# First attention of block 1: each head's scores made by themselves, with the value products between the two heads

## The chip, the cores and the metric

The kernel runs on one core of one Trainium2 chip. The metric is device time in microseconds (us) of one execution, taken as the median of several runs. The core has a matmul engine (PE, with PEld for its weight loads), a vector engine (DVE), a scalar engine (ACT), GpSimd (POOL) and a queue for transfers (SP). They run their own instruction streams in order and meet at semaphores.

## The reference, cut to what matters

The program computes a first transformer block (with three mixing branches) and two further layers, in float32, for 512 tokens of width 1024. The change lies in branch "a" of the first block: attention in a window, with 8 query heads of width 64 that share 2 key heads, over blocks of 128 queries. A block of queries sees 256 context keys, and of the sequence its own block of 128 keys and its neighbours, masked to a distance of 128, and one "sink" score per head:

```python
s_loc = jnp.einsum('bnqkgd,bnjkd->bkgnqj', qb, kb).astype(jnp.float32) * scale
s_loc = jnp.where(valid, s_loc, NEG_BIG)
s_ctx = jnp.einsum('bnqkgd,bjkd->bkgnqj', qb, ck).astype(jnp.float32) * scale
p = jax.nn.softmax(jnp.concatenate([s_ctx, s_loc, s_sink], axis=-1), axis=-1).astype(v.dtype)
o = (jnp.einsum('bkgnqj,bjkd->bnqkgd', p[..., :n_ctx], cv)
     + jnp.einsum('bkgnqj,bnjkd->bnqkgd', p[..., n_ctx:n_ctx + 3 * BLOCK], vb))
```

## The kernel before, in words

The program is a row of stages. In a stage each engine has its stream, written by hand as a Python function (`tensor`, `scalar`, `vector`, `gpsimd`), and the order of the calls in it is the order on the engine. `paired_attention` makes one such stage. `attend("A", ...)` (windowed) is the stage that the change touches, `attend("B", ...)` (every query sees all 768 keys) comes straight after it with the same function, and a third use of the function, `slots=2`, is the latent attention of the later layers.

A unit `u` is a pair of heads (g = 0 and 1) and one block tb of 128 queries; there are 4 pairs and 4 blocks, so 16 units, `u = 4 * pair + tb`. The pair's two heads lie in partitions 0 to 63 and 64 to 127 of the queries `qkA` and keys `kA`. For A, units with tb = 0 or 3 have 512 keys and one masked block (narrow units here), units with tb = 1 or 2 have 640 keys and two masked blocks (wide units). Per unit:

- `scores(u)` on PE: for each range of key columns one matmul of head 0 and one of head 1, in turn, into eight banks' first half: head 0 has PSUM banks 0 and 1, head 1 has banks 2 and 3. There is room for one unit, so it waits until both heads' exponentials of the unit before are done. One semaphore step, `scored`, tells of both heads.
- `maxima(u)` on DVE: for head 0 and then head 1, add the mask (line 1163), put the sink score in (line 1165), take the row maximum (line 1167).
- `exps(u)` on ACT: exponential and row sum of head 0, then of head 1 (line 1139), out of the banks into `probsA`.
- `inverses(u)` on DVE (line 1172) waits for both exponentials; POOL then scales both heads' probabilities (line 1210).
- `transposes(u)` on PE (line 1092) turns the probabilities into banks 4, 5, 6, and `copies` brings them to `probsTA`: banks 4 and 6 by ACT (line 1144), bank 5 by DVE (line 1129).
- `values(u)` on PE (line 1105) waits for all three copies, and multiplies with the values into bank 7. After the fourth unit of a pair DVE reads bank 7 out (line 1179).

The streams are, for each u in turn: PE `scores(u+1)`, `values(u-1)`, `transposes(u)`; DVE `inverses(u)`, `maxima(u+1)`, after a pair's first unit the readout of the pair before, then its copy of unit u; ACT `exps(u+1)`, then its two copies of unit u.

Of the kernel before, what the change touches and what calls it, by code (L numbers as in the profile page):

```python
# [121 lines left out]
def build_program(nc, stream, xT_in, ctxT_in, memT_in, pos_in, const_in, axial_in, par1_in, par2_in, out):  # L122
    stack = ExitStack()
    with stack:
# [33 lines left out]
        def p1(name, n=1, at=0):  # L158
            return par1[:, PAR1[name] + at:PAR1[name] + at + n]
# [882 lines left out]

            stage(name, tensor=tensor, scalar=scalar, vector=vector, gpsimd=gpsimd)

        def paired_attention(name, pairs, unit_of, read_out, work, slots, turn_banks, out_banks, copier, sink=None):


            units = [unit_of(t, tb) for t in range(pairs) for tb in range(TB)]
            N = len(units)
            G = len(turn_banks)  # L1050
            scored = Signal("scored", N)
            max_ready = Signal("max_ready", 2 * N)
            exp_done = Signal("exp_done", 2 * N)
            inverse_ready = Signal("inverse_ready", N)
# [18 lines left out]
            def tensor(pe):  # L1073
                def scores(u):
                    if u >= slots:
                        pe.wait_ge(exp_done.sem, exp_done.at(2 * (u - slots + 1)))
                    for lo, hi, operands in units[u]["scores"]:
                        for g in range(2):
                            lhsT, rhs = operands[g]
                            last = nc.tensor.matmul(head_scores(u, g)[:, lo:hi], lhsT, rhs, start=True, stop=True)  # L1080
                    last.then_inc(scored.sem, 1)

                def transposes(u):
                    keys = units[u]["keys"]
                    for b in range(G):
                        if u > 0:
                            pe.wait_ge(probs_out[b].sem, probs_out[b].at(u))
                        for n, x in enumerate(turned_tiles(u, b)):
                            g, j = divmod(x, keys)
                            if j == 0:  # L1090
                                pe.wait_ge(probs_ready.sem, probs_ready.at(2 * u + g + 1))
                            last = nc.tensor.transpose(bank[:, turn_banks[b], n * P:(n + 1) * P],
                                                       probs[:, u % 2, g, j * P:(j + 1) * P], con("ident"))
                        last.then_inc(turned[b].sem, 1)

                def values(u):
                    t, tb = divmod(u, TB)
                    if tb == 0 and t >= len(out_banks):
                        pe.wait_ge(sum_read.sem, sum_read.at(t - len(out_banks) + 1))
                    for b in range(G):  # L1100
                        pe.wait_ge(probs_out[b].sem, probs_out[b].at(u + 1))
                    keys = units[u]["keys"]
                    for j, sides in enumerate(units[u]["values"]):
                        for g in range(2):
                            last = nc.tensor.matmul(bank[g * HD:(g + 1) * HD, out_banks[t % len(out_banks)], tb * P:(tb + 1) * P],
                                                    sides[g], probsT[:, u % 2, (g * keys + j) * P:(g * keys + j + 1) * P],
                                                    start=j == 0, stop=j == keys - 1)
                    if tb == TB - 1:
                        last.then_inc(summed.sem, 1)

                scores(0)
                if slots == 2:
                    scores(1)
                for u in range(N + 1):
                    if u + slots < N:
                        scores(u + slots)
                    if slots == 1 and u >= 1:
                        values(u - 1)
                    if u < N:
                        transposes(u)  # L1120
                    if slots == 2 and u >= 1:
                        values(u - 1)
# [32 lines left out]

            def vector(dve):
                def maxima(u):
                    dve.wait_ge(scored.sem, scored.at(u + 1))
                    unit = units[u]
                    for g in range(2):  # L1160
                        S = head_scores(u, g)
                        for lo, mask in unit["masks"]:
                            nc.vector.tensor_tensor(S[:, lo:lo + P], S[:, lo:lo + P], mask, ALU.add)
                        if sink:
                            nc.vector.tensor_copy(S[:, unit["width"] - 1:unit["width"]], sink(u // TB, g))
                            dve.drain()
                        nc.vector.tensor_reduce(stat[:, u % 2, 0, g:g + 1], S[:, 0:unit["width"]], AX.X, ALU.max, negate=True)\
                            .then_inc(max_ready.sem, 1)

                def inverses(u):  # L1170
                    dve.wait_ge(exp_done.sem, exp_done.at(2 * (u + 1)))
                    nc.vector.reciprocal(stat[:, u % 2, 2, :], stat[:, u % 2, 1, :]).then_inc(inverse_ready.sem, 1)  # L1172

                def dve_copies(u):
                    copies(dve, "dve", u, nc.vector.tensor_copy)

                def turn_out(t):
                    dve.wait_ge(summed.sem, summed.at(t + 1))
                    nc.vector.tensor_copy(read_out(t), bank[:, out_banks[t % len(out_banks)], :]).then_inc(sum_read.sem, 1)

                nc.vector.memset(stat[:, :, :, :], 0.0)
                dve.drain()
                maxima(0)
                if slots == 2:
                    inverses(0)
                    maxima(1)
                    for u in range(N):
                        if u + 1 < N:
                            inverses(u + 1)
                        if u + 2 < N:  # L1190
                            maxima(u + 2)
                        dve_copies(u)
                        if u % TB == 1 and u > TB:
                            turn_out(u // TB - 1)
                else:
                    for u in range(N):
                        inverses(u)
                        if u + 1 < N:
                            maxima(u + 1)
                        if u % TB == 0 and u:  # L1200
                            turn_out(u // TB - 1)
                        dve_copies(u)
                turn_out(pairs - 1)
# [1091 lines left out]
        def attend(which, b, windowed, qk, k, v):  # L2295

                with ExitStack() as a:
                    work = (same_place(f"probs{which}", "hcT", [P, 2, 2, ALLT], F32), tmp(f"probsT{which}", [P, 2, 2 * ALLT], a),
                            tmp(f"stat{which}", [P, 2, 3, 2], a))

                    def unit_of(n, tb):
                        lo, hi = (max(0, tb - 1), min(TB, tb + 2)) if windowed else (0, TB)
                        width = CT + (hi - lo) * P
                        key_cols = [(0, CT, 0), (CT, min(width, 512), CT + lo * P)] if lo else [(0, 512, 0)]
                        if width > 512:
                            key_cols.append((512, width, 512 + lo * P))
                        masks = []
                        if windowed and lo < tb:
                            masks.append((CT, con("mask_prev")))
                        if windowed and hi > tb + 1:  # L2310
                            masks.append((width - P, con("mask_next")))
                        blocks = list(range(CB)) + [CB + x for x in range(lo, hi)]
                        rows = [slice(g * HD, (g + 1) * HD) for g in range(2)]
                        return dict(scores=[(a0, a1, [(qk[r, n, tb * P:(tb + 1) * P], k[r, s0:s0 + a1 - a0]) for r in rows])
                                            for a0, a1, s0 in key_cols],
                                    width=width + (1 if windowed else 0), masks=masks, keys=width // P,
                                    values=[[v[:, x, r] for r in rows] for x in blocks])
                    paired_attention(f"attend{which}", 4, unit_of, lambda n: yab[:, b, n, :], work, 1, (4, 5, 6), (7,),
                                     ("act", "dve", "act"),
                                     sink=(lambda n, g: p1("sink", 1, n + 4 * g)) if windowed else None)  # L2320


        with ExitStack() as s:
# [104 lines left out]
            work = {}  # L2428
# [848 lines left out]
```

## Time and profile before

| | |
|---|---|
| median of 3 runs | 3217.31 us (3217.26 to 3220.99) |
| profiled execution, its own time | 3217.78 us |
| its span in the profile | 3216.0 us |
| PE busy | 2983.4 us, 93% of the span |
| DVE, ACT, POOL busy | 1520.6, 1281.8, 327.6 us |
| stage A | from 489.01 us (first scores) to 572.05 us (last readout ends) |
| stage B | from 572.37 us to 654.24 us |

Time in the trace is counted from the start of the span. A fp32 matmul stands in the trace as two records, and a transpose as one. Busy times of PE are modelled, so a group's duration reaches a little past the start of the next. The granted clock (PEclk) is a share of the full rate: 1.00 is 2.4 GHz, 0.50 is 1.2 GHz.

### The profile page before, as it was taken

The page shows a single profiled execution, that of the slowest core. Times are in us where ns is not written, and L with a number is a line of the kernel's source. Part 1 is how long each engine was busy: PE and PEld are TensorE (multiplying, and loading weights), DVE is VectorE, ACT ScalarE, POOL GpSimd, SP SyncE. Part 2 cuts the span into 40 slices and gives each one's busy share as a digit, 9 for nine tenths or more (in the row PEclk, how much of TensorE's full clock was granted, in tenths as well). Part 3 has the DMA queues.
Part 4 walks back from the last instruction along what each step waited for, and adds up shares of the span by engine and source line. Part 5 has one row for each costly group of instructions (what it writes and reads, how often), then busy time and mean ns, then how long its engine had stood idle before and what let it go on. Part 6 is the DMA issues. An engine that isn't in the chain of part 4 may idle for free. (4 is left out here: it accounts for less than half of the span.)

```text
span 3216.0 us, 39342 instructions
## 1 busy us (share of the span) xinstructions
PE 2983.4 (93%) x14872; PEld 2330.9 (72%) x14872; DVE 1520.6 (47%) x2141; ACT 1281.8 (40%) x1866; POOL 327.6 (10%) x285
## 2 busy tenths in 40 slices
PE   6989897899989999899899989999899899899998
PEld 2879775678768888576577768887675577678885
DVE  3346346555544442356643354442465563354432
ACT  3751334532233332434553343333434653433333
POOL 0010003500001100003000111100104001011100
PEclk8999999999999999999799999999999899999999
DMA  6100210045422222120022112222120131122222
GB/s 230 66 27 1 73 66 1 2 133 177 161 74 96 91 104 92 62 79 14 27 105 92 53 66 95 101 101 79 67 79 1 49 123 53 53 92 94 103 101 79
DMA packets 43556, 254.09 MB, mean 79 GB/s; under 512 B 4608, under 2 KB 6784, under 8 KB 15872
## 3 DMA queue, kind: packets, MB, share of 16 engines
q1 hardware_dynamic: 43392, 251.87, 21.9%
q8 instruction: 107, 1.75, 0.2%
q14 instruction: 57, 0.47, 0.0%
HBM read 249.75 MB, written 2.10 MB: 78 GB/s over the span
## 5 line engine op out<-in xcount | busy, mean ns | idle before, releaser
L238 DVE TENSOR_TENSOR ring_lo<-ring,ring_hi 128x2048 fp32r<-128x2048 f32 x201 | 460.7, 2292 | 881.5 <-ACT ring_hi L231 881.5
L289 PE MATMUL bank<-h_hi,ring_hi 128*128 128x512 f32 x1360 | 557.2, 410 | 17.2 <-DVE mix_lo L1588 6.4
L231 ACT ACTIVATE ring_hi<-ring 128x2048 fp32r<-128x2048 f32 x201 | 383.8, 1910 | 463.2 <-PE bank L289 343.3
L289 PE MATMUL bank<-h_hi,ring_lo 128*128 128x512 f32 x1360 | 534.1, 393 | 0.0
L1402 PE MATMUL bank<-h_hi,ring_hi 128*128 128x512 f32 x960 | 374.1, 390 | 5.7 <-DVE ring_lo L238 5.7
L1405 PE MATMUL bank<-h_lo,ring_hi 128*128 128x512 f32 x960 | 373.5, 389 | 0.0
L1406 PE MATMUL bank<-h_hi,ring_lo 128*128 128x512 f32 x960 | 373.5, 389 | 0.0
L289 PEld LDWEIGHTS bank<-h_hi,ring_hi 128*128 128x128 f32 x1360 | 257.2, 189 | 86.3 <-issue 22.1
L289 PEld LDWEIGHTS bank<-h_hi,ring_lo 128*128 128x128 f32 x1360 | 257.0, 189 | 60.0
L289 PE MATMUL bank<-h_lo,ring_hi 128*128 128x512 f32 x624 | 243.8, 391 | 0.0
L1402 PEld LDWEIGHTS bank<-h_hi,ring_hi 128*128 128x128 f32 x960 | 180.2, 188 | 45.3 <-issue 5.5
L289 PE MATMUL bank<-gated_lo,ring_hi 128*128 128x512 f32 x528 | 209.3, 396 | 0.0
L1406 PEld LDWEIGHTS bank<-h_hi,ring_lo 128*128 128x128 f32 x960 | 180.2, 188 | 37.5
L1405 PEld LDWEIGHTS bank<-h_lo,ring_hi 128*128 128x128 f32 x960 | 180.2, 188 | 37.4
L1510 DVE SCALAR_TENSOR_TENSOR mix<-bank,par,mix 128x511 f32<-128x511 f32 x176 | 123.8, 745 | 130.6 <-ACT mix L1466 124.3
L289 PEld LDWEIGHTS bank<-h_lo,ring_hi 128*128 128x128 f32 x624 | 117.8, 189 | 27.6 <-issue 3.9
L1466 ACT ACTIVATE mix<-bank,par 128x512 f32<-128x512 f32 x88 | 63.7, 774 | 150.2 <-PE bank L1406 150.2
L289 PE MATMUL bank<-mix_lo,ring_hi 128*128 128x512 f32 x272 | 116.5, 428 | 6.0 <-PEq L337 6.0
L289 PEld LDWEIGHTS bank<-gated_lo,ring_hi 128*128 128x128 f32 x528 | 99.2, 188 | 24.4 <-issue 2.4
L1532 POOL TENSOR_TENSOR gated<-mix 128x512 f32 (+1 forms) x44 | 57.2, 1299 | 425.9 <-ACT mix L1471 425.9
L1210 POOL TENSOR_TENSOR squares<-squares,stat 128x512 f32<-128x512 f32 x64 | 65.3, 1041 | 331.5 <-DVE stat L1172 331.5
L1510 DVE SCALAR_TENSOR_TENSOR conv<-bank,par,conv 128x511 f32<-128x511 f32 x88 | 61.9, 745 | 65.5 <-ACT conv L1466 62.4
(449 smaller groups left out, 5089.0 us busy)
## 6 DMA issues: line engine op xcount, KB each, us to landing
ring<-in_stream SPq DMA_DIRECT2D x209, 1024.0 KB, 4.8
mod_w<-in_stream SPq DMA_DIRECT2D x64, 256.0 KB, 4.8
xT<-in_xT SPq DMA_DIRECT2D x2, 2048.0 KB, 14.8
const<-in_const SPq DMA_DIRECT2D x1, 2306.5 KB, 16.0
par<-in_par SPq DMA_DIRECT2D x3, 696.0 KB, 3.9
memT<-in_memT SPq DMA_DIRECT2D x2, 1024.0 KB, 4.9
out<-xT SPq DMA_DIRECT2D x1, 2048.0 KB, 6.3
ctxT<-in_ctxT SPq DMA_DIRECT2D x1, 1024.0 KB, 4.8
```

The lines of the kernel that those rows point to most:

```text
L231: nc.scalar.activation(self.slab_hi(slab + j), self.slab(slab + j), ACT.Copy).then_inc(slab_rounded, 1)
L238: nc.vector.tensor_tensor(lower, self.slab(slab + j), self.slab_hi(slab + j).bitcast(F32), ALU.subtract)\
L289: ins = nc.tensor.matmul(out, lhsT, rhs, start=start and w is w_hi and x is x_hi, stop=stop and w is w_lo)
L1210: nc.gpsimd.tensor_tensor(p, p, stat[:, u % 2, 2, g:g + 1].to_broadcast([P, p.shape[1]]), ALU.mult)\
L1402: first = nc.tensor.matmul(out_ap[s], w_hi, x_hi, start=k == 0, stop=False)
L1405: nc.tensor.matmul(out_ap[s], w_hi, x_lo, start=False, stop=False)
L1406: last = nc.tensor.matmul(out_ap[s], w_lo, x_hi, start=False, stop=k == KT - 1)
L1466: last = nc.scalar.activation(work[:, j % 2, s, :], out_ap[s], ACT.Identity, bias=conv_b(col), scale=conv_w(2 * FT + col))
L1510: last = nc.vector.scalar_tensor_tensor(w, out_ap[s][:, 1 - lo:T - lo], conv_w(col), w, ALU.mult, ALU.add)
L1532: nc.gpsimd.tensor_tensor(gated(n), work[:, j % 2, 0, :], work[:, j % 2, 1, :], ALU.mult)\
```

## The change

With `apart` set (stage A alone), each head's scores are a step of their own, `head_alone(u, g)`. It waits only for that head's exponential of the unit before, and signals that head alone; DVE waits per head. PE's order for each u becomes: head 0 of unit u+1, values of u-1, head 1 of unit u+1, transposes of u.

```diff
-            scored = Signal("scored", N)
+            scored = Signal("scored", 2 * N if apart else N)
...
+                def head_alone(u, g):
+                    if u >= 1:
+                        pe.wait_ge(exp_done.sem, exp_done.at(2 * (u - 1) + g + 1))
+                    for lo, hi, operands in units[u]["scores"]:
+                        lhsT, rhs = operands[g]
+                        last = nc.tensor.matmul(head_scores(u, g)[:, lo:hi], lhsT, rhs, start=True, stop=True)
+                    last.then_inc(scored.sem, 1)
+
+                if apart:
+                    head_alone(0, 0)
+                    head_alone(0, 1)
+                else:
+                    scores(0)
                 if slots == 2:
                     scores(1)
                 for u in range(N + 1):
-                    if u + slots < N:
+                    if apart and u + 1 < N:
+                        head_alone(u + 1, 0)
+                    if u + slots < N and not apart:
                         scores(u + slots)
                     if slots == 1 and u >= 1:
                         values(u - 1)
+                    if apart and u + 1 < N:
+                        head_alone(u + 1, 1)
                     if u < N:
                         transposes(u)
...
-                    dve.wait_ge(scored.sem, scored.at(u + 1))
+                    if not apart:
+                        dve.wait_ge(scored.sem, scored.at(u + 1))
                     unit = units[u]
                     for g in range(2):
+                        if apart:
+                            dve.wait_ge(scored.sem, scored.at(2 * u + g + 1))
                         S = head_scores(u, g)
...
-                                     sink=(lambda n, g: p1("sink", 1, n + 4 * g)) if windowed else None)
+                                     sink=(lambda n, g: p1("sink", 1, n + 4 * g)) if windowed else None, apart=windowed)
```

On PE at the third and fourth unit of a pair, before (kA and qkA are the scores, probsTA the values, probsA the transposes):

```order
L1080 MATMUL bank<-kA,qkA 128x256 x4
L1080 MATMUL bank<-kA,qkA 128x128 x2
L1105 MATMUL bank<-probsTA,vab 64x128 x8
L1092 MATMUL bank<-const,probsA 128x128 x10
L1080 MATMUL bank<-kA,qkA 128x256 x4
L1105 MATMUL bank<-probsTA,vab 64x128 x10
L1092 MATMUL bank<-const,probsA 128x128 x10
```

and the same units with the change:

```order
L1117 MATMUL bank<-kA,qkA 128x256 x2
L1117 MATMUL bank<-kA,qkA 128x128
L1106 MATMUL bank<-probsTA,vab 64x128 x8
L1117 MATMUL bank<-kA,qkA 128x256 x2
L1117 MATMUL bank<-kA,qkA 128x128
L1093 MATMUL bank<-const,probsA 128x128 x10
L1117 MATMUL bank<-kA,qkA 128x256 x2
L1106 MATMUL bank<-probsTA,vab 64x128 x10
L1117 MATMUL bank<-kA,qkA 128x256 x2
L1093 MATMUL bank<-const,probsA 128x128 x10
```

The same matmuls are issued, but head 1's moved behind the values of the unit before. At the start of the stage PE had

```order
L1080 MATMUL bank<-kA,qkA 128x512 x4
L1080 MATMUL bank<-kA,qkA 128x128 x2
L1092 MATMUL bank<-const,probsA 128x128 x8
L1080 MATMUL bank<-kA,qkA 128x256 x4
L1080 MATMUL bank<-kA,qkA 128x128 x2
```

and has with the change

```order
L1117 MATMUL bank<-kA,qkA 128x512 x3
L1117 MATMUL bank<-kA,qkA 128x128
L1117 MATMUL bank<-kA,qkA 128x512
L1117 MATMUL bank<-kA,qkA 128x128
L1093 MATMUL bank<-const,probsA 128x128 x8
```

The first three are both heads of unit 0 and head 0 of unit 1; no values stand between the heads yet, since there is no unit before. DVE, ACT and POOL issue the same instructions in the same order as before; DVE only has one more wait in each unit.

## Rows read from the trace of the kernel before

**Rows 1.** The page: busy time, share and instructions of each engine.

```profile
PE 2983.4 (93%) x14872; PEld 2330.9 (72%) x14872; DVE 1520.6 (47%) x2141; ACT 1281.8 (40%) x1866; POOL 327.6 (10%) x285
```

**Rows 2.** Stretches of stage A: length, busy us (instructions), clock, DMA share, GB/s.

```profile
489.00:494.00 5.00, 1.93 (x6) 0.81 (x8) 2.25 (x8) 2.81 (x5) 0.57 (x1) 0.74 0.00 0
...
494.00:572.00 78.00, 59.12 (x556) 44.35 (x552) 48.97 (x141) 36.65 (x92) 35.47 (x32) 0.93 0.00 1
...
499.00:504.00 5.00, 4.46 (x29) 3.56 (x30) 2.03 (x9) 1.50 (x5) 2.47 (x2) 0.50 0.00 0
```

**Rows 3.** Who waited for whom in stage A: us, times, longest.

```profile
PE bank L1080 <- ACT probsA L1139: 19.3, 15, 3.1
DVE bank L1163 <- PE bank L1080: 20.3, 16, 2.4
```

**Rows 4.** Timeline, 520 to 536 us: start, us, engine, line, what [idle before].

```profile
520.89 0.50 DVE L1163 TENSOR_TENSOR bank<-bank,const 128x128 f32<-128x128 f32 x2 [1.24 <-PE bank L1080]
...
522.26 0.49 DVE L1163 TENSOR_TENSOR bank<-bank,const 128x128 f32<-128x128 f32 x2
...
523.74 0.80 ACT L1139 ACTIVATE probsA<-bank,statA 128x641 f32<-128x641 f32 x1 [0.42 <-DVE statA L1167]
...
524.53 0.86 ACT L1144 ACTIVATE probsTA<-bank 128x512 f32<-128x512 f32 x2
...
524.68 1.14 PE L1080 MATMUL bank<-kA,qkA 64*128 64x256 f32 x8 [1.57 <-ACT probsA L1139]
...
525.75 1.31 PE L1105 MATMUL bank<-probsTA,vab 128*64 128x128 f32 x20
525.86 0.30 DVE L1163 TENSOR_TENSOR bank<-bank,const 128x128 f32<-128x128 f32 x1 [1.03 <-PE bank L1080]
...
526.90 0.29 DVE L1163 TENSOR_TENSOR bank<-bank,const 128x128 f32<-128x128 f32 x1
...
526.99 1.31 PE L1092 MATMUL bank<-const,probsA 128*128 128x128 f32 x10
...
528.05 0.69 ACT L1139 ACTIVATE probsA<-bank,statA 128x513 f32<-128x513 f32 x1 [0.19 <-DVE statA L1167]
...
528.73 0.86 ACT L1144 ACTIVATE probsTA<-bank 128x512 f32<-128x512 f32 x2
...
532.93 0.76 ACT L1144 ACTIVATE probsTA<-bank 128x384 f32<-128x384 f32 x2
...
533.09 1.35 PE L1080 MATMUL bank<-kA,qkA 64*128 64x512 f32 x8 [0.80 <-ACT probsA L1139]
...
534.37 1.09 PE L1105 MATMUL bank<-probsTA,vab 128*64 128x128 f32 x16
534.48 0.50 DVE L1163 TENSOR_TENSOR bank<-bank,const 128x128 f32<-128x128 f32 x2 [1.25 <-PE bank L1080]
...
535.39 1.09 PE L1092 MATMUL bank<-const,probsA 128*128 128x128 f32 x8
```

**Rows 5.** Timeline, the last units of the stage.

```profile
565.64 0.69 ACT L1139 ACTIVATE probsA<-bank,statA 128x513 f32<-128x513 f32 x1 [0.19 <-DVE statA L1167]
...
566.32 0.86 ACT L1144 ACTIVATE probsTA<-bank 128x512 f32<-128x512 f32 x2
...
567.33 1.31 PE L1105 MATMUL bank<-probsTA,vab 128*64 128x128 f32 x20 [1.44 <-ACT probsTA L1144]
```

**Rows 6.** Timeline, the first units of the stage.

```profile
489.01 1.13 PE L1080 MATMUL bank<-kA,qkA 64*128 64x512 f32 x4 [1.66 <-PEq L337]
...
491.33 0.69 ACT L1139 ACTIVATE probsA<-bank,statA 128x513 f32<-128x513 f32 x1 [1.09 <-DVE statA L1167]
...
492.37 0.69 ACT L1139 ACTIVATE probsA<-bank,statA 128x513 f32<-128x513 f32 x1 [0.25 <-DVE statA L1167]
...
493.20 2.50 PE L1080 MATMUL bank<-kA,qkA 64*128 64x512 f32 x8 [3.06 <-ACT probsA L1139]
```

**Rows 7.** Timeline, latent attention: one head's scores, keys in all 128 partitions.

```profile
1502.43 1.98 PE L1080 MATMUL bank<-hT,q 128*128 128x512 f32 x4
```

More of the change, by code:

```diff
@@ L1043, in attention, with paired_attention @@
             stage(name, tensor=tensor, scalar=scalar, vector=vector, gpsimd=gpsimd)
-        def paired_attention(name, pairs, unit_of, read_out, work, slots, turn_banks, out_banks, copier, sink=None):
+        def paired_attention(name, pairs, unit_of, read_out, work, slots, turn_banks, out_banks, copier, sink=None, apart=False):
             units = [unit_of(t, tb) for t in range(pairs) for tb in range(TB)]
@@ L1109, in values @@
                         last.then_inc(summed.sem, 1)
-                scores(0)
+                def head_alone(u, g):
[10 more added lines that the diff above has]
+                    scores(0)
                 if slots == 2:
```

## The prediction

> **What bounds the kernel now.** I read the page first: PE is busy for 93% of the span and no other engine for half of it [rows 1]. The change touches stage A alone, so the second view is the busy time of that stage. There PE is busy for 59.12 of 78 us [rows 2]: it is not at its limit, and the stage is set by a chain of waits through three engines. The waits name it: PE's scores wait for ACT's exponential 15 times, 19.3 us in all, and DVE's first mask waits for PE's scores 16 times, 20.3 us [rows 3]. The timeline shows the chain [rows 4]. From a wide unit's exponential of head 1 (523.74) it goes to the next scores (524.68), from these to the first mask (525.86), through both heads on DVE (the masks start at 525.86 and 526.90) and to the next exponential of head 1 (528.05). The values (525.75) and transposes (526.99) run on PE while DVE works, and cost nothing. What follows stage A waits for its end, so what the stage loses or gains goes to the total in full.
>
> The chain in pieces, N for a narrow unit and W for a wide one. Exponential of head 1 to the next scores: 0.94 W (523.74 to 524.68), 0.83 N (492.37 to 493.20) [rows 4, 6]. Scores to mask: 1.18 N (524.68 to 525.86), 1.39 W (533.09 to 534.48). DVE's head 0: 1.04 N (525.86 to 526.90), 1.37 W (520.89 to 522.26). DVE's head 1 until ACT starts: 1.15 N (526.90 to 528.05), 1.48 W (522.26 to 523.74) [rows 4]. From one wide unit to the next this gives 0.94 + 1.39 + 1.37 + 1.48 = 5.18 us, and four units of a pair give 18.7.
>
> **What the change does, part by part.**
>
> *The two heads are no longer side by side.* A head takes 64 of the array's 128 rows. Two matmuls of 512 columns (four records), one in each half, take 1.13 us in stage A [rows 6]; the same four records with keys in all 128 rows take 1.98 us in the latent attention [rows 7]. So in stage A the halves work at once, and the difference, 0.85 us, is one whole matmul. I take it that a head by itself costs the 0.85 us (640 columns: 1.07) that both cost now, so that PE's work on scores doubles; half of that is the lower bound, and a rival below. "Scores to mask" then stays at 1.18 and 1.39 for one head.
>
> *Head 0 goes ahead.* Its scores for unit u+1 need only the exponential of head 0 of unit u, and PE has nothing else then (it waits there now). DVE can start its head 0 right behind `inverses(u)`. So DVE's head 0 (1.04 or 1.37) leaves the chain. That is the gain.
>
> *Head 1 goes behind the values of u-1.* On PE `values(u-1)` stands ahead of head 1, and it waits for the copies of u-1. ACT issues those behind both exponentials of unit u. Queued behind this wait on PE are head 1 and the transposes of u; DVE's head 1, ACT's exponential of head 1 and all that follows wait for head 1. The new chain, from exponential of head 1 to exponential of head 1, is:
> - exponential to ACT's copies: 0.68 N (528.05 to 528.73), 0.79 W (523.74 to 524.53); the two copies of the unit before take 0.76 N or 0.86 W [rows 4];
> - last copy to values: the end of the stage has this already, since no scores are left there. The copies start at 566.32 and take 0.86, the values start at 567.33, so 0.15 [rows 5];
> - values to the next group on PE: 1.02 N (534.37 to 535.39), 1.24 W (525.75 to 526.99) [rows 4];
> - scores to mask of the next unit, 1.18 or 1.39, and DVE's head 1, 1.15 or 1.48.
>
> By position in the pair (the copies and values are those of the unit before):
> - unit 0 to 1: 0.68 + 0.76 + 0.15 + 1.02 + 1.39 + 1.48 = 5.48
> - 1 to 2: 0.79 + 0.76 + 0.15 + 1.02 + 1.39 + 1.48 = 5.59
> - 2 to 3: 0.79 + 0.86 + 0.15 + 1.24 + 1.18 + 1.15 = 5.37
> - 3 to 0: 0.68 + 0.86 + 0.15 + 1.24 + 1.18 + 1.15 = 5.26
>
> Four units: 21.7 against 18.7 now. 14 of the 15 steps are of this kind: 4 x 5.59 + 4 x 5.37 + 3 x 5.26 + 3 x 5.48 = 76.1 us. The first step has no values in it. Head 0's exponential starts at 491.33 [rows 6], head 0 of unit 1 goes at 491.33 + 0.83 = 492.16, DVE has it at 493.55, head 1 at 494.92, and the exponential comes at 496.40: 4.0 us from 492.37. Together 80.1 us. Now it is 492.37 [rows 6] to 565.64 [rows 5], 73.3 us. Behind the last exponential nothing changes. The stage is **6.8 us longer**.
>
> *An array that changes its tiling once more per unit.* Values and the following group are 1.24 us apart where the values' modelled time is 1.31 [rows 4], so 0.07 overlaps; that 1.24 is in the sum. The Trainium skill ("TensorEngine Tiling (Array Packing)", Key Properties) says that changing the tiling mode drains the engine. With a full drain the step would be 1.31, and the sum 14 x 0.07 = 1.0 us more; the trace has it at 1.24, and I keep that.
>
> *The clock at the start.* PE waits 3.06 us after the first scores, and the second ones take 2.50 us [rows 6] against 1.35 later for the same shapes [rows 4]: the clock has fallen to its lower level, 1.2 GHz (0.74 on average from 489 to 494, 0.50 from 499 to 504) [rows 2]. With the change PE works for 1.7 us first, then waits some 1.3 us instead of 3.06. The sum above has the full clock throughout. So it already has in it that the half clock, which now costs two steps 1.15 us each, goes away. If the clock falls all the same, both heads of unit 1 lie one behind the other on the chain, and each takes 1.15 more: about 2.2 us on top. If it stays low for another unit, its values (1.0) and head 1 (1.15) add the next 2.1.
>
> *The rest.* DVE's added waits cost nothing: each is over when DVE comes to it, or it is head 1's, counted above. POOL's scaling starts where it did, with `inverses(u)`, and the transposes now come later than it. Transfers are idle in the stage (1 GB/s) [rows 2].
>
> **The sum.** The profiled execution took 3217.78 us and would take 3224.6. It lies 0.47 over the median of 3217.31; from that: 3217.3 + 6.8 = **3224.1 us**.
>
> **The rivals.**
> - *The clock falls anyway* (0.34). For: a wait of over 1 us is still there and PE idles before the stage. Against: it is less than half as long as the one now. 3224.1 + 2.2 = 3226.3, up to 3228.4.
> - *A head alone takes half as long as two* (0.10), if it isn't the halves working at once that the 1.13 against 1.98 shows but matmuls of 64 rows being quicker. Then "scores to mask" falls by 0.43 N and 0.53 W, over 14 steps 6.7 us, and 0.5 in the first: 6.8 - 7.2 = -0.4, 3216.9 us. Against: the Trainium skill ("TensorE: Matmul & The Clock Gate", table "Why this matters for your kernels") says that a single matmul of 32 rows takes the time of one of 128, and that the gain is the tiles' concurrency.
> - *Not slower, since the values don't stand in the way* (0.05). If the values of u-1 had run before the exponential of head 1 of unit u ended, head 1 would start at once, and PE's own row would be the limit: per narrow unit two heads of 1.07 (524.68 to 525.75) and twice 1.02, per wide unit two of 1.28 (533.09 to 534.37) and twice 1.24, or 18.4 for four against 18.8 measured. That gives some 1.3 us, with the 2.3 of the clock 3.6: 3213.7. It decides where the copies and values take 6.8 / 14 = 0.5 us less of each step. Against: ACT's copies are in its stream behind both exponentials.
> - *More is late than I count* (0.05): a transpose or readout that now holds up head 0, 0.5 us per unit: 3232.
>
> **How the numbers follow.** My forecast holds 0.46. It is a sum of 14 equal steps, so 0.1 us in a step is 1.4 in the total; its own range is 3222 to 3226.5. A measurement of this kernel tells about 0.2% from no change, 6.4 us, so the line is at 3223.7. The forecast lies close to it: 0.6 of its share is slower; of the clock rival 0.9; of the last all. 0.46 x 0.6 + 0.34 x 0.9 + 0.05 = 0.63 slower. Faster by over 6.4 us has no mechanism above, only errors of several together: 0.04. The rest, 0.33, is within. For the range I leave out the half-time rival's lower part and the last: 3217 to 3229.
>
> **What would show it.** In the changed profile: a head's scores of 512 columns in about 1.1 us and 640 in 1.3; values that start 0.15 us behind ACT's copies, with the idle time put down to them; head 1's first mask waiting for PE, head 0's not; 21.7 us per pair; PE's busy time in the stage up by about 15 us; the clock at 1.00 from 492 to 500. I am wrong if head 1's scores start right at the exponential's end, if a head's scores take half, or if DVE's head 0 still waits.

## The result, and the profile after

The changed kernel takes 3227.6 us in the median of its first eight runs, against 3217.3 (3215.3 to 3221.0) for the kernel before: 0.33% slower, with a 95% interval of 0.24 to 0.43%. Seven of the eight lie between 3225.2 and 3232.3 us (median 3227.3); the eighth, a slow one at a granted clock of 0.525, took 7940 us and is left out of the comparison. Run again beside the experiments it took 3226.0 (3225.4 to 3227.9), 0.30% slower (0.19 to 0.42).

The page of the changed kernel, its span and the busy time of the engines:

```profile
span 3226.2 us, 39342 instructions
...
PE 3002.6 (93%) x14872; PEld 2343.1 (73%) x14872; DVE 1521.2 (47%) x2141; ACT 1281.4 (40%) x1866; POOL 327.6 (10%) x285
```

Beside [rows 1]: the same instructions, and PE busy for 19.2 us more (its weight loads, PEld, for 12.2 us more). The busy times of DVE, ACT and POOL have not moved by a microsecond.

The timeline of the changed kernel, at the end of a pair and the start of the next. Line 1117 is one head's scores, 1106 the values, 1093 the transposes; on ACT line 1156 is the exponential and 1161 the copies; on DVE line 1183 is the mask.

```profile
531.70 1.31 PE L1106 MATMUL bank<-probsTA,vab 128*64 128x128 f32 x20 [1.02 <-ACT probsTA L1161]
532.11 0.69 ACT L1156 ACTIVATE probsA<-bank,statA 128x513 f32<-128x513 f32 x1 [0.55 <-DVE statA L1187]
...
532.94 1.13 PE L1117 MATMUL bank<-kA,qkA 64*128 64x256 f32 x4
...
534.00 1.31 PE L1093 MATMUL bank<-const,probsA 128*128 128x128 f32 x10
...
534.11 0.30 DVE L1183 TENSOR_TENSOR bank<-bank,const 128x128 f32<-128x128 f32 x1 [2.09 <-PE bank L1117]
...
535.24 1.12 PE L1117 MATMUL bank<-kA,qkA 64*128 64x512 f32 x2
535.26 0.69 ACT L1156 ACTIVATE probsA<-bank,statA 128x513 f32<-128x513 f32 x1 [2.38 <-DVE statA L1187]
535.94 0.86 ACT L1161 ACTIVATE probsTA<-bank 128x512 f32<-128x512 f32 x2
...
536.40 0.30 DVE L1183 TENSOR_TENSOR bank<-bank,const 128x128 f32<-128x128 f32 x1 [0.16 <-PE bank L1117]
...
536.95 1.31 PE L1106 MATMUL bank<-probsTA,vab 128*64 128x128 f32 x20 [0.59 <-ACT probsTA L1161]
...
538.19 1.12 PE L1117 MATMUL bank<-kA,qkA 64*128 64x512 f32 x2
```

Read it as a chain from 535.26. ACT's exponential of head 1 starts. Its copies start at 535.94 and end at 536.80. The values start at 536.95, 0.15 behind, and PE's idle time is put down to those copies. Head 1's scores start at 538.19, 1.24 behind the values. One head's 512 columns, two records, take 1.12 us, where both heads' four records took 1.13 in [rows 6]. DVE's mask of head 0 waits for 0.16 us (536.40), that of head 1 for 2.09 (534.11). The exponentials of head 1 come at steps of 5.48, 5.59, 5.35 and 5.25 us through a pair, 21.7 us, against 18.8 before.

Who waited for whom in stage A of the changed kernel, from 489 to 582 us (us in all, times, longest):

```profile
DVE bank L1183 <- PE bank L1117: 32.9, 24, 2.9
PEld bank L1106 <- ACT probsTA L1161: 12.1, 10, 1.8
...
PE bank L1106 <- ACT probsTA L1161: 10.7, 13, 1.6
...
PE bank L1117 <- ACT probsA L1156: 2.0, 1, 2.0
```

Beside [rows 3], PE's scores no longer wait for the exponential (19.3 us then, 2.0 now), but PE's values wait for ACT's copies (10.7 us), and DVE waits longer than before for scores (32.9 against 20.3).

The first units, and two stretches of the stage with the granted clock (the third figure from the end):

```profile
488.87 1.13 PE L1117 MATMUL bank<-kA,qkA 64*128 64x512 f32 x4 [1.66 <-PEq L337]
...
491.99 3.53 PE L1117 MATMUL bank<-kA,qkA 64*128 64x512 f32 x8 [1.99 <-ACT probsA L1156]
```

```profile
492.00:511.00 19.00, 19.00 (x79) 14.04 (x80) 8.21 (x25) 6.52 (x16) 6.97 (x6) 0.50 0.00 0
516.00:582.00 66.00, 55.94 (x434) 40.04 (x430) 37.43 (x108) 28.44 (x72) 27.73 (x25) 1.00 0.01 1
```

The first scores take 1.13 us, as before: unit 0 has one range per head, so its two matmuls stand in the same order as they did. PE still idles 1.99 us ahead of unit 1, the clock falls to 1.2 GHz near 491.3, and it stays there until about 511.6 although PE is busy in all of those 19 us. In the kernel before it was back near 505. The steps there are 5.2, 8.3 and 7.9 us, where the chain at the full clock has 4.0, 5.6 and 5.4.

From stage A's first scores to stage B's first scores it is 83.4 us before (489.01 to 572.37) and 96.5 after (488.87 to 585.33): 13.1 us longer. I call this "stage A" below. The span grew by 10.2 only. Of the difference 1.7 us comes back in a later stage whose code is the same (its place is 12.5 us late before it and 10.8 after it). The windows of that place, 13 us apart, the kernel before first:

```profile
847.00:867.00 20.00, 17.75 (x75) 14.17 (x74) 12.89 (x17) 8.67 (x12) 0.00 (x0) 0.91 0.50 189
```

```profile
860.00:880.00 20.00, 17.75 (x80) 14.24 (x80) 12.91 (x18) 9.08 (x12) 0.00 (x0) 1.00 0.49 188
```

The clock fell there for a moment before the change, and doesn't now. The rest of the program wanders by more than this: outside stage A the profiled execution has 3132.6 us before, 3129.7 in the changed kernel and 3127.2 in its second profile, and over all kernels below 3123.0 to 3134.9. So stage A itself is the better measure of each experiment.

### The profile page after: what moved, and what is told of

Read it like the earlier page. It is cut to its first block and busy times, and to the rows that moved or that the text cites. A ratio compares the mean times of both kernels' runs of the same rounds, so it can differ in the third digit from the quotient of the medians.

```text
span 3226.2 us, 39342 instructions
## 1 busy us (share of the span) xinstructions
PE 3002.6 (93%) x14872; PEld 2343.1 (73%) x14872; DVE 1521.2 (47%) x2141; ACT 1281.4 (40%) x1866; POOL 327.6 (10%) x285
```

## The experiments

Theory A, of the prediction: the values between the heads, with their wait for ACT's copies, make the chain longer than DVE's head 0 shortens it, and the low clock at the start adds to it. Theory B: the scores' doubled work on PE is the cause, wherever the values stand.

Stage A is read from the one profiled execution of each kernel, the median from all its runs; the interval compares them with runs of the kernel before made beside them.

| kernel | stage A | median, us | against before, 95% interval |
|---|---|---|---|
| before | 83.4 | 3217.3 | |
| changed | 96.5 | 3227.6 | +0.24 to +0.43% |
| changed, again | 96.5 | 3226.0 | +0.19 to +0.42% |
| both heads ahead of the values | 74.9 | 3208.1 | -0.50 to -0.23% |
| the same with a filler | 70.7 | 3205.3 | -0.52 to -0.25% |
| the same, heads staggered by one range | 72.6 | 3202.1 | -0.57 to -0.30% |
| changed with a filler | 90.0 | 3227.4 | +0.17 to +0.41% |
| before with fillers | 82.9 | 3214.9 | -0.14 to +0.04% |
| before, head after head | 87.8 | 3221.6 | +0.06 to +0.26% |
| both ahead, head 0 waits for both exponentials | 86.1 | 3216.4 | -0.12 to +0.07% |
| before, values first | 131.6 | 3263.6 (one run) | |
| changed with filler, copies between | 80.9 | 3220.2 | -0.02 to +0.20% |

### Both heads ahead of the values

```diff
                     if apart and u + 1 < N:
                         head_alone(u + 1, 0)
+                        head_alone(u + 1, 1)
...
                     if slots == 1 and u >= 1:
                         values(u - 1)
-                    if apart and u + 1 < N:
-                        head_alone(u + 1, 1)
```

> The changed kernel, but both heads' scores of unit u+1 stand ahead of the values of u-1 (head 0, head 1, values, transposes). Theory A (the values between the heads, with their wait for ACT's copies, make the chain long): the chain shrinks to 13.9 us per four units and PE's own row of 18.4 sets the pace, so stage A takes 78 us at the full clock (before 83.0, changed 96.1); if the clock stays low as long as in the changed kernel, 85 to 88. In total 3213 to 3222. Theory B (the doubled scores on PE cost the time, wherever the values stand): stage A stays at 90 or more at the full clock, 3224 or more in total.

It took 3208.1 us (3200.7 to 3208.7), 0.36% under the kernel before, and stage A 74.9 us. In the full-clock part the steps are 3.9 to 4.6 us, 16.2 for four units. Theory B's 90 us for the stage is out, since only the values have moved. But 16.2 is also under the 18.4 that I had as PE's own limit, and stage A was below the 78 expected. The timeline of this kernel shows why:

```profile
524.94 1.37 PE L1117 MATMUL bank<-kA,qkA 64*128 64x512 f32 x4
...
526.24 1.31 PE L1106 MATMUL bank<-probsTA,vab 128*64 128x128 f32 x20
...
527.48 1.09 PE L1093 MATMUL bank<-const,probsA 128*128 128x128 f32 x8
...
528.29 0.69 ACT L1155 ACTIVATE probsA<-bank,statA 128x513 f32<-128x513 f32 x1 [0.20 <-DVE statA L1186]
...
528.50 1.97 PE L1117 MATMUL bank<-kA,qkA 64*128 64x512 f32 x8
...
530.40 1.09 PE L1106 MATMUL bank<-probsTA,vab 128*64 128x128 f32 x16
```

Both heads of a narrow unit take 1.30 us from start to the values (524.94 to 526.24), not twice 1.07. When nothing stands between the heads, head 1's matmul, which uses the array's other half, runs beside the rest of head 0's. A wide unit takes 1.90 us (528.50 to 530.40), not twice 1.28; its head 1 cannot start with head 0, since it waits for ACT's exponential, which starts at 528.29 and takes 0.69. The values in between take that away as well, so this run alone does not part the values' wait from the longer scores; the run with the copies moved, below, does. From 516 to 553 PE is busy for 36.98 of 37 us. It has no idle time left, but head 1's wait still lies inside its order.

```profile
516.00:553.00 37.00, 36.98 (x317) 28.91 (x316) 29.69 (x86) 21.57 (x57) 20.47 (x18) 1.00 0.00 1
```

### The clock at the start: a filler

```diff
                 if apart:
                     head_alone(0, 0)
                     head_alone(0, 1)
+                    for _ in range(1):
+                        nc.tensor.matmul(bank[:, 7, :], con("ident"), yc[:, 0, :], start=True, stop=True)
```

The filler writes into a bank that the stage overwrites before it is read. In the changed kernel:

> The changed kernel with one matmul of 128 rows and 512 columns more, whose result nobody uses, behind the first two heads' scores, where PE idles. Theory A: of the 13.1 us that stage A is longer, 6.8 are the chain and 6.3 the clock at 1.2 GHz from 491.4 to 511.6; if the filler keeps the clock up, stage A takes 89.9 us, with a step of 5.6 from unit 1 to unit 2 instead of 8.3, and the total is 3221 to 3225. If the first steps are long for another reason than the clock, the steps stay at 5.2 and 8.3 and stage A at 96 even with the clock at 1.00. If the clock falls in spite of the filler, the run tells nothing.

The first rows of stage A in that kernel, and the clock over its whole length:

```profile
490.25 1.12 PE L1124 MATMUL bank<-yc,const 128*128 128x512 f32 x2
...
492.31 2.38 PE L1117 MATMUL bank<-kA,qkA 64*128 64x512 f32 x8 [0.94 <-ACT probsA L1158]
```

```profile
489.20:503.20 14.00, 11.80 (x64) 7.36 (x64) 9.06 (x29) 7.17 (x16) 4.51 (x4) 1.00 0.00 0
503.20:579.20 76.00, 63.04 (x498) 45.20 (x499) 42.50 (x122) 32.27 (x82) 31.54 (x28) 1.00 0.00 1
```

The clock stays up (1.00), and the first scores of unit 1 take 2.38 us where they took 3.53. The steps are 4.04, 5.58, 5.36, 5.25, 5.47 and so on, each within 0.02 us of the prediction's, and stage A takes 90.0 us, 6.7 more than before. So of the 13.1 us, 6.7 are the chain and 6.4 the low clock. The median, 3227.4 us (3222.8 to 3230.1), lies above the 3221 to 3225 expected: what stage A gave back (6.4 us) does not show in the total. In the profiled execution the rest of the program took 4.3 us more than in the changed kernel's (3134.0 against 3129.7). The stage with the clock's dip alone took 4.5 us more: its place 855 to 955 us of the kernel before lasts 102.7 us here and 98.2 in the changed kernel. Two later places, 4.9 us shorter and 5.1 us longer, nearly cancel.

In the kernel with both heads ahead of the values:

> The first kernel of this set with one filler. Theory A: with the full clock PE's row of 18.4 us per four units sets the pace: stage A 78.3 us, total 3211 to 3214, so 0.1 to 0.2% under the kernel before. Theory B: stage A 90.

Stage A 70.7 us, 3205.3 us (3204.2 to 3207.4). All steps are 3.9 to 4.5. Of the 4.3 us less in the stage, 4.1 are in the first four steps, where the low clock had been. It is 12 us, 0.38%, under the kernel before, and better than expected for the reason above.

In the kernel before, three of them behind the first `scores`:

> The kernel before with three such fillers behind the first scores of stage A (the gap there is 3.1 us). Theory A: the half clock costs the kernel before 2.3 us in its first steps, so stage A takes 80.7 us instead of 83.0 and the total is 3214 to 3216. If the clock's cost is hidden: 83.0 and no change.

Stage A took 82.9 us and 3214.9 in total (3214.6 to 3217.8), no measurable change. The first step got shorter (6.23 to 5.08 us) but the second stayed at 6.34, and one later went from 5.19 to 5.92: the clock fell later instead (1.00 from 490 to 495, but 0.86 from 495 to 500, 0.75 from 520 to 525 and 0.70 from 540 to 545). The fillers only moved it, so this run doesn't tell the price that I had named (2.3 us).

### The heads' places alone

```diff
-                    for lo, hi, operands in units[u]["scores"]:
-                        for g in range(2):
-                            lhsT, rhs = operands[g]
+                    spans = units[u]["scores"]
+                    for i, g in [(i, g) for g in range(2) for i in range(len(spans))] if sink else \
+                            [(i, g) for i in range(len(spans)) for g in range(2)]:
+                        lo, hi, operands = spans[i]
+                        lhsT, rhs = operands[g]
```

> The kernel before, but scores() of stage A issues all ranges of head 0 and then all of head 1, instead of one of each in turn; waits, the one signal and the place ahead of the values stay. It measures what is lost when the heads don't stand side by side. If matmuls of the two halves overlap only where they are next to each other in PE's order, then head 0's last range and head 1's first still overlap: units with one range per head lose nothing, units with two or three lose 0.4 to 0.9 us each, 2.1 per four units, 8 in all: stage A 91, total 3223 to 3227. If two heads in turn don't run at once at all (half-time rival): no change, 3217. If a head alone takes the full time with no overlap: 15 us more, 3232.

3221.6 us (3218.4 to 3225.7), stage A 87.8. The total is just under the range, but the mechanism that I had given, a loss in every unit with two or three ranges, is wrong in its detail. The scores of this kernel, all at the full clock, for units with two ranges (twice), and with three:

```profile
525.28 1.14 PE L1082 MATMUL bank<-kA,qkA 64*128 64x256 f32 x8 [0.17 <-ACT probsA L1141]
...
533.70 1.36 PE L1082 MATMUL bank<-kA,qkA 64*128 64x512 f32 x8 [0.80 <-ACT probsA L1141]
...
538.90 1.89 PE L1082 MATMUL bank<-kA,qkA 64*128 64x256 f32 x12 [1.80 <-ACT probsA L1141]
```

With two ranges per head the time is what it was with the heads in turn (1.14 and 1.35 in [rows 4]), although two matmuls of head 0 stand ahead of head 1's first. The trace's single records show how: two records of 512 columns start together (533.70 and 533.71), and all four come before the first of 128 columns (534.66). So head 1's first matmul ran ahead of head 0's second, which stands before it in PE's order. With three it is 1.89 against the 1.36 that the same 12 records took before: 0.5 us lost, once in four units. That is 2 us in the stage; I put the other 2.4 down to dips of the clock (0.83 from 520 to 530, 0.73 from 560 to 570, where it was 1.00 before).

### Head 0's early start alone

```diff
                 def head_alone(u, g):
                     if u >= 1:
-                        pe.wait_ge(exp_done.sem, exp_done.at(2 * (u - 1) + g + 1))
+                        pe.wait_ge(exp_done.sem, exp_done.at(2 * u))
```

on top of the kernel with both heads ahead of the values.

> The kernel with both heads ahead of the values, but head 0 too waits for both exponentials of the unit before; DVE still gets a signal per head. The doubled work on PE is there, the early start of head 0 is not. If the early start is what gave the 9.6 us of the kernel with no values between: steps as in the kernel before (5.2, 4.3, 4.2, 5.1), stage A 83, total 3216 to 3219. If it were the signal per head or the changed order: near 3208.

3216.4 us (3210.9 to 3218.9), no difference from the kernel before, and steps of 5.17, 4.30, 4.19, 5.06 where the clock is up. So neither the signal per head nor the new order gives anything; the early start of head 0 gives all of what the kernel with both heads ahead gained. Its stage A of 86.1 is 2.7 us longer than before, which I put down to lower clocks (0.63 from 500 to 510 against 0.75, and 0.66 from 540 to 545 against 1.00). The profiled execution is the fastest of its ten, 3210.9 us, by a rest of the program of 3123.0 us.

### The values' place alone

```diff
                 for u in range(N + 1):
+                    if sink and u >= 1:
+                        values(u - 1)
                     if u + slots < N:
                         scores(u + slots)
-                    if slots == 1 and u >= 1:
+                    if slots == 1 and u >= 1 and not sink:
                         values(u - 1)
```

> The kernel before with heads side by side, but with the values of u-1 ahead of the scores of u+1 in stage A (values, scores, transposes). It measures the place of the values alone. Theory A: the wait for ACT's copies and the values stand in the chain, with DVE's head 0 still in it: steps of 7.0, 6.4, 6.3, 6.9 instead of 5.2, 4.3, 4.2, 5.1, stage A 110, total 3244. If the values' place cost little and the doubled scores were the cause: below 3222.

3263.6 us in its one run, stage A 131.6. It is in the direction of Theory A and far beyond its number: the steps are 6.2 to 9.0. The chain (7.0, 6.4, 6.3, 6.9) was worked out at the full clock. Here the clock comes and goes, 0.73 on average in the stage against 0.92 before, and PE waits for ACT's copies 16 times, 41.9 us in all. How much of the miss is the clock was not measured.

```profile
548.81 1.31 PE L1105 MATMUL bank<-probsTA,vab 128*64 128x128 f32 x20 [2.68 <-ACT probsTA L1146]
550.05 1.13 PE L1080 MATMUL bank<-kA,qkA 64*128 64x512 f32 x4
...
554.99 1.98 PE L1105 MATMUL bank<-probsTA,vab 128*64 128x128 f32 x16 [2.79 <-ACT probsTA L1146]
```

The second values take 1.98 us for 16 records, 1.09 in [rows 4]: the half clock. The wait on ACT's copies is in both rows.

### The copies' place

In the changed kernel with a filler, ACT's two copies of unit u-1 go between its exponentials of unit u.

```diff
                     for g in range(2):
+                        if apart and g == 1 and u >= 1:
+                            act_copies(u - 1)
...
-                    if slots == 1:
+                    if slots == 1 and not (apart and u + 1 < N):
                         act_copies(u)
```

> The changed kernel with one filler, and with ACT's copies of unit u-1 moved between its two exponentials of unit u, so that the values don't wait for copies behind head 1's exponential. Theory A: the values start earlier, but ACT then waits for the transposes; four units take 20.3 us instead of 21.7, stage A 85, total 3220 to 3223. If the wait for the copies is not what holds the values: steps unchanged at 5.6, 5.4, 5.3, 5.5 and 3225 to 3228.

Stage A took 80.9 us, 9.1 less than the same kernel without this (90.0), with steps of 4.4 to 5.2 and 19.1 for four units, better than the 20.3 expected. The median is 3220.2, but the runs spread from 3212.9 to 3227.3, and the profiled one took 3217.7; the total can't be told from the kernel before. What holds the changed kernel is shown all the same. The order on PE is that of the changed kernel, head, values, head, with each head by itself, so its work is as large. PE is busy for 75.0 us of the stage, against 74.9 without the moved copies. Only the copies come earlier, the values hardly wait for ACT any more, and the chain is 2.5 us shorter in four units:

```profile
PE bank L1106 <- ACT probsTA L1165: 0.6, 1, 0.6
```

```profile
520.00:530.00 10.00, 10.00 (x73) 6.37 (x74) 6.28 (x18) 5.73 (x15) 4.50 (x4) 1.00 0.01 2
530.00:540.00 10.00, 9.49 (x73) 7.25 (x71) 7.32 (x21) 5.19 (x13) 4.50 (x4) 1.00 0.00 1
```

So it is the wait, and not PE's work, that sets the changed kernel's pace. But the work is close behind. Without the wait PE is busy for 19.49 of 20 us (520 to 540), and four units take 19.1 us, still not under the 18.8 of the kernel before. The kernel with both heads ahead takes 16.2, and with a filler its PE is busy for 66.7 us of the stage, since the heads overlap there. Of the 5.5 us per four units between the changed kernel and that one, 2.5 are the wait, and the other 2.9 come when the heads are neighbours.

### Staggered heads

On top of the kernel with both heads ahead and a filler: head 0's first range, then one range of each head in turn (still behind the two waits), then head 1's last. For a unit with one or two ranges per head this list is the same as without, so only the units with three ranges, one in four, change their order.

> The kernel with both heads ahead of the values and one filler (3205.3 us, four units in 16.2 us, PE never idle), but head 1 now stands one range behind head 0 in PE's order instead of a whole head: first range of head 0, then in turn a range of each, then the last of head 1. Theory A (PE sets the pace and matmuls of the two halves overlap when they are next to each other): units with two or three ranges per head take 0.4 us less on PE, so four units take 15.2 to 15.8 us, 2 to 4 us in all: 3201 to 3204. If head 1's wait for its exponential holds up head 0's second range, or the chain of 13.9 us with DVE is already the limit: no change or 1 us slower.

3202.1 us (3201.4 to 3205.7), but stage A is 72.6 us, 1.9 longer than without (70.7), with steps of 4.54, 3.30, 4.54, 4.29, 16.7 for four units. In the stage the expectation failed, and its own second case came out: head 1's wait for its exponential holds up what stands behind it. The unit with three ranges gets shorter, from its scores to its values, only from 2.51 to 2.35 us. The next unit, whose order on PE is the same, gets longer, from 1.46 (534.28 to 535.74) to 2.05 us (533.84 to 535.89). Without and with the staggered order:

```profile
534.28 1.53 PE L1117 MATMUL bank<-kA,qkA 64*128 64x256 f32 x8
...
535.74 1.31 PE L1106 MATMUL bank<-probsTA,vab 128*64 128x128 f32 x20
```

```profile
533.84 2.12 PE L1130 MATMUL bank<-kA,qkA 64*128 64x256 f32 x8
535.89 1.31 PE L1106 MATMUL bank<-probsTA,vab 128*64 128x128 f32 x20
```

So PE's work alone does not set the pace of these kernels. The lower total has its cause outside the stage (3127.0 us against 3132.8 in the profiled executions), and the intervals of the two kernels overlap. Both beat the kernel before.

### The changed kernel again

> The changed kernel once more, beside the others on one chip, to see how far its time and the clock at the start of stage A repeat: 3225 to 3232, stage A 96 with a step of 8 us or more where the clock is low, 90 where it isn't.

Stage A took 96.5 us again, with a second step of 8.32, and the same stretch of 19 us at the half clock:

```profile
489.60:508.60 19.00, 19.00 (x79) 14.04 (x80) 8.10 (x25) 6.52 (x16) 6.97 (x6) 0.50 0.00 0
```

So the low clock at the start is no accident of one run. The span is 3223.7 us, only 7.7 more than before.

## Why the prediction was right, and where it was off

**The chain.** Right in every piece. Predicted steps 5.48, 5.59, 5.37, 5.26; measured 5.48, 5.59, 5.35, 5.25. Last copy to values 0.15, values to head 1 1.24, each as read from the kernel before. Predicted 6.8 us in all; 6.7 with the clock held up.

**A head alone costs what two cost.** Right for the changed kernel: two records in 1.12 us. The half-time rival is out.

**The clock.** The step that failed is the choice between my forecast and the clock rival. I took it that 1.7 us of work and a shorter idle time would hold the clock up. The 1.7 was a misreading: unit 0's two matmuls stand in the same order as before and took 1.13 us as before, so PE idled 1.99 us (I had 1.3), and the clock fell. The sign that I had named, a clock of 1.00 from 492 to 500, did not come; it was 0.50. The rival's price was also too small: 2.2, or 4.3 us if it stayed low for another unit, against the 6.4 measured, since it stayed low for 20 us with PE busy.

**The total.** 3224.1 was forecast, within 3217 to 3229, and 3227.6 measured. The right sum would have been 6.7 + 6.4 = 13.1, less 2.9 that the rest of the program gave back, 1.7 of it shown as a dip of the clock that is gone. I had written that all of the stage's loss goes to the total; in the second profile, with the same 96.5 us, the rest was 5.4 us shorter. That the error is only 3.5 us is in part luck, since the clock's 6.4 and the rest's 2.9 have opposite signs.

**The rival on the other side.** "Not slower, since the values don't stand in the way" did not come true in the changed kernel. The two kernels that make its condition true bear it out. With the copies moved, and the heads still apart, PE is all but always busy and four units take 19.1 us, close to the 18.4 that I had as PE's own limit. With the values behind both heads that limit no longer holds, since the heads overlap: four units take 16.2 us, and the total is 3208.1, well under the rival's 3213.7.

**PE's busy time** in stage A rose from 61.05 to 82.21 us, 21.2 instead of the 15 expected. With the clock held up it is 74.86, the filler's 1.1 included. So some 13 us are the heads' doubled work and some 8 the longer stretch at the half clock.

## What to carry to other kernels

Starting a piece of work as soon as its own input is there pays only if nothing that waits for something later stands between it and the next piece: here 0.33% lost turned into 0.36% won when the values went behind both heads. Of the 5.5 us per four units between the two kernels, 2.5 are the wait; the rest came with the heads being neighbours. When an in-order engine gets a new item ahead of a critical one, write down that item's own last wait (here copies queued behind another engine's critical work) and add it to the chain. The matmuls of the two heads, in different halves of the array, cost one time only while they were near neighbours in the order: 1.36 us for both heads of 640 columns in two ranges, against 1.34 us for each (531.31 in the kernel with the copies moved) when the values stood between them.

## What was not expected of the hardware

- One head's matmuls overlap the other head's across two matmuls in PE's order (1.14 and 1.36 us for both heads in turn or one after the other), but not fully across three (1.89 against 1.36 us). With two ranges the heads' first records start 0.01 us apart (533.70 and 533.71), out of PE's order; with three, 0.54 us apart (538.90 and 539.44).
- The clock stayed at 1.2 GHz for 20 us while PE was busy all the time, in both profiles of the changed kernel (19.00 of 19.00 us, clock 0.50). With one matmul of 128 rows in the first gap it stayed at 1.00 through the stage. What makes the difference was not settled. In that stretch the scores use half of the array's rows at a time, which was not tried by itself.
- Fillers in a gap can move a fall of the clock to a later place and gain nothing (83.4 to 82.9 us).
